# Order of gather, scatter, column copies and result scaling in the routed-expert loop of a hybrid encoder block

## The chip, the cores and the metric

One core of a Trainium2 chip runs the whole kernel. The metric is the device time in microseconds (us) of one execution: the median of three runs of the kernel before is 1347.29 us (1344.2 to 1349.36). One more execution was profiled; all rows below are of that one.

## The reference, cut to what matters

The block is one encoder layer on 512 tokens of width 1024 in float32: a token mixer (recurrent branch and differential attention) and then a mixture of experts (MoE). The change touches only the MoE. There each token is routed to 8 of 64 experts, and their weighted outputs are added up:

```python
    _, eidx = lax.top_k(sel, TOP_K)                      # 8 of 64 experts for each of 512 tokens
    w = jnp.take_along_axis(s, eidx, axis=-1)
    w = w / jnp.sum(w, axis=-1, keepdims=True) * ROUTED_SCALE
    gate = jnp.sum(jax.nn.one_hot(eidx, N_EXPERTS) * w[..., None], axis=1)
    ...
        hg = jnp.einsum('nd,edf->nef', tk, we_gate)      # 1024 -> 256
        hu = jnp.einsum('nd,edf->nef', tk, we_up)
        act = jax.nn.silu(hg) * hu * gk[..., None]
        return jnp.einsum('nef,efd->nd', act, we_down)   # 256 -> 1024
    ...
    ffn = routed + shared
    x = _layer_norm(ALPHA * x + g2[:, None, :] * ffn, ln2_g, ln2_b)
```

## The kernel before

The kernel computes only the (token, expert) pairs that were routed. They are packed into **units** of 128 rows (`Item` in the code): two halves of 64 rows, each half for one expert. Here there are 52 units, counted 0 to 51, and two units make a pair. Everything that has two buffers (`x_rows`, `y_item`, `row_index`, `y_index`, `places`, `columns`, `pick`) is used by even and odd units in turn.

What happens to unit i, engine by engine:

- GpSimd (POOL), `expert_columns` (L742, L743): copies the two experts' columns of the routing table (`places`, `columns`). The numbers of the experts come from the plan, read into registers by `Plan.move_on` (L420, L421) once for each pair.
- VectorE (DVE), `pick_tokens` (L2005): builds a 0/1 matrix that says which token sits in which row.
- TensorE (PE), `pick_slots` (L1118): multiplies it with the columns. This leaves in PSUM bank 7 the token number, the number of the result's row and the weight of each row.
- DVE, `token_index` (L2016): writes `row_index`. POOL, `gather` (L721): one indirect DMA brings the 128 token rows (4 KB each, 512 KB in all) from DRAM into `x_rows`.
- DVE, `token_weight` (L2026, L2027): copies the other numbers out of bank 7. Only then may PE run `pick_slots` of the next unit (semaphore `slots_read`), since it overwrites bank 7.
- PE, `transpose_rows` (L1127); ScalarE (ACT) takes the result out of PSUM; PE, `gate_up` (L1139); DVE, `activate` (L2048).
- DVE, `result_index` (L2054): writes `y_index`, the rows of DRAM that the results go to. As this buffer was last used by unit i-2, it waits until the scatter of unit i-2 has landed (semaphore `y_scattered`).
- PE, `project_down` (L1161); DVE, `result_out` (L2062): multiplies by g2 out of PSUM into `y_item`. POOL, `scatter` (L731): one indirect DMA writes the 128 result rows (512 KB) to DRAM.

The engines run these as a software pipeline. In step i (one turn of the loop) PE does, in this order: the transposes of the activations of unit i-1 (L1147), `pick_slots` of i+2, `transpose_rows` of i+1, `gate_up` of i, `project_down` of i-1. Each engine takes its instructions strictly in the order in which they are written, and waits where a semaphore isn't there yet. The orders around the change are written out by hand in the `step` functions of POOL (L763) and DVE (L2096); `over_items` (L457) calls them twice for each turn of a loop, an even unit and then an odd one. The loop's branch and `plan.move_on` stand ahead of the even unit.

The weights of the experts (3 MB each, 64 experts) come from DRAM through the queue of SyncE (SP), into a ring of four buffers. Gather and scatter both go through POOL's queue.

Of the kernel before, what the change touches and what calls it, by code (L numbers as in the profile page):

```python
# [119 lines left out]
def hybrid_block(nc, x, c, w_ada, b_ada, w_in, conv_w, conv_b, lru_w_a, lru_b_a, lru_w_i, lru_b_i, lru_lambda,  # L120
# [3 lines left out]
    with ctx:  # L124
# [255 lines left out]
        def bcast(row, at_axis, n):  # L380

            a = row.unsqueeze(at_axis)
            return a.broadcast_to([n if k == at_axis else d for k, d in enumerate(a.shape)])
# [57 lines left out]
        def wait(engine, semaphore, value):  # L441

            if not isinstance(value, int) or value > 0:
                engine.wait_ge(semaphore, value)

        def value_of(engine, value):

            return value if isinstance(value, int) else engine.snap(value)

        def count_of(engine, place, least, most):  # L450

            count, held = engine.alloc_register(f"count{place}"), engine.alloc_register(f"held{place}")
            engine.reg_load(held, items[0:1, place:place + 1])
            engine.reg_alu(count, held, least, ALU.max)
            return engine.snap(count, min_val=least, max_val=most)

        def over_items(engine, step, plan):  # L457


            pairs = count_of(engine, PAIRS, MIN_PAIRS, MAX_PAIRS)  # L460
            for par in range(2):
                step(Item(0, par, plan), par == 0, False, False)
            with engine.Fori(1, pairs - 1) as pair:
                if plan:
                    plan.move_on(pair)
                for par in range(2):
                    step(Item(pair, par, plan), False, False, False)
            if plan:
                plan.move_on(pairs - 1)
            for par in range(2):  # L470
                step(Item(pairs - 1, par, plan), False, par == 1, True)
            return Item(pairs - 1, 1, plan)
# [177 lines left out]
        def _(pool):  # L650
# [56 lines left out]
            def settle():  # L707

                pool.reg_alu(last_row, last_row, T - 1, ALU.min)
# [5 lines left out]
            def gather(item):  # L715
                indexed, transposed = value_of(pool, item.n + 1), value_of(pool, item.n - 1)
                pool.wait_ge(rows_stored, 16 * NT)
                wait(pool, index_ready, indexed)
                wait(pool, x_tr, transposed)
                settle()  # L720
                pool.indirect_dma_start(out=x_rows[item.par][:, :], out_offset=None, in_=u_rows,  # L721
                                        in_offset=bass.IndirectOffsetOnAxis(ap=row_index[item.par][:, 0:1], axis=0),
                                        bounds_check=last_row, oob_is_err=False).then_inc(rows_gathered[item.par], 16)

            def scatter(item):
                projected = value_of(pool, item.n + 1)
                pool.wait_ge(rows_stored, 16 * NT)
                wait(pool, yindex_ready, projected)
                wait(pool, y_out, projected)
                pool.reg_alu(last_result, last_result, T * TOPK - 1, ALU.min)  # L730
                pool.indirect_dma_start(out=y_rows, in_=y_item[item.par][:, :], in_offset=None,  # L731
                                        out_offset=bass.IndirectOffsetOnAxis(ap=y_index[item.par][:, 0:1], axis=0),
                                        bounds_check=last_result, oob_is_err=False
                                        ).then_inc(y_scattered[item.par], 16)

            def expert_columns(item):

                wait(pool, pick_done, item.n - 1)
                for h in range(2):
                    expert = item.expert(h)  # L740
                    settle()
                    nc.gpsimd.tensor_copy(places[item.par][:, :, h:h + 1], place[:, :, bass.ds(expert, 1)])  # L742
                    last = nc.gpsimd.tensor_copy(columns[item.par][:, :, h:h + 1, :], table[:, :, bass.ds(expert, 1), :])  # L743
                last.then_inc(columns_ready, 1)
# [9 lines left out]
            plan = Plan(pool, (ITEM_E,), 0, 4)  # L754
# [6 lines left out]
            expert_columns(Item(0, 2, plan))  # L761

            def step(item, first, last, end):  # L763
                if not end:

                    gather(item.ahead(2))
                    expert_columns(item.ahead(3))
                if not first and not (end and item.par):
                    scatter(item.ahead(-1))

            over_items(pool, step, plan)

            for t in range(NT - 1):
                last_rstd(2 * NT + t)
# [731 lines left out]
        def _(dve):  # L1506
# [493 lines left out]
            def pick_tokens(item):  # L2000

                wait(dve, columns_ready, item.n + 1)
                wait(dve, pick_done, item.n - 1)
                wait(dve, slot_step, item.n)
                V.tensor_tensor(pick[item.par][:, :, :].rearrange("p t (h s) -> p t h s", h=2),  # L2005
                                bcast(slot_id[:, :].rearrange("p (h s) -> p h s", h=2), 1, NT),
                                bcast(places[item.par][:, :, :], 3, HP), ALU.is_equal).then_inc(pick_ready, 1)
                wait(dve, pick_ready, item.n + 1)
                V.tensor_scalar(slot_id[:, :], slot_id[:, :], float(P), None, ALU.add).then_inc(slot_step, 1)

            def token_index(item):
                wait(dve, pick_done, item.n + 1)
                wait(dve, rows_gathered[item.par], item.pair * 16)
                for h in range(2):
                    rows = slice(h * HP, (h + 1) * HP)
                    last = V.tensor_scalar(row_index[item.par][rows, :], bank[7][rows, COLUMNS * h:COLUMNS * h + 1], float(SKIP),  # L2016
                                           None, ALU.add)
                last.then_inc(index_ready, 1)
# [14 lines left out]
            def take_gu(item):  # L2033
                wait(dve, gu_half, item.n * 2 - 1)
                for h in range(2):
                    load = item.load(h)
                    dve.wait_ge(gu_in[0], load * 32 + 32)
                    slot = slot_of(dve, slot_reg, load)
                    for b in range(2):
                        last = V.tensor_copy(gu_use[h][:, b, 0:KD // 2, :],  # L2040
                                             gu[:, bass.ds(slot, 1), b, 0:KD // 2, :].rearrange("p o k n -> p (o k) n"))
                    last.then_inc(gu_first, 1)

            def activate(item):

                wait(dve, silu_ready, item.n + 1)
                wait(dve, acted_tr, item.n)
                V.scalar_tensor_tensor(out=acted[:, :], in0=bank[item.par][:, DE:2 * DE],  # L2048
                                       scalar=picked[item.par][:, 1:2], in1=silu[:, :], op0=ALU.mult,
                                       op1=ALU.mult).then_inc(acted_ready, 1)  # L2050
# [6 lines left out]
            def result_out(item):  # L2057
                wait(dve, y_done, item.n + 1)
                wait(dve, y_scattered[item.par], item.pair * 16)
                for half in range(2):  # L2060
                    cols = slice(half * 512, (half + 1) * 512)
                    last = V.tensor_tensor(y_item[item.par][:, cols], bank[5 + half][:, :], g2_row[:, cols], ALU.mult)  # L2062
                last.then_inc(y_out, 1)
# [17 lines left out]
            plan = Plan(dve, (ITEM_L,), 0, 2)  # L2081
# [12 lines left out]
            shared_in_x1(1)  # L2094

            def step(item, first, last, end):  # L2096
                if not end:
                    token_index(item.ahead(2))
                    pick_tokens(item.ahead(3))
                if not last:  # L2100
                    take_gu(item.ahead(1))
                activate(item)
                result_index(item)
                if not end:
                    token_weight(item.ahead(2))
                if last:
                    scale_shared()
                if not first:
                    result_out(item.ahead(-1))

            last_item = over_items(dve, step, plan)
            wait(dve, y_done, last_item.n)
            load = last_item.load(1)
            dve.wait_ge(down_in, load * 16 + 16)
# [124 lines left out]
```

## Time and profile before

| | |
|---|---|
| median of three runs | 1347.29 us |
| the profiled execution | 1348.29 us |
| its span, first to last instruction | 1346.6 us |
| mean granted TensorE clock | 0.989 |
| units in the expert loop | 52 |
| PE busy in the span | 96% |
| DVE, ACT, POOL busy | 59%, 52%, 14% |

The loop over the experts fills the stretch from about 645 us to 1290 us. Times in the rows are microseconds from the start of the span; durations marked as a mean of one are nanoseconds. In a row of the timeline the bracket at the end tells how long the engine had been idle and who ended the wait. "issue" there is time of the engine's own sequencer: register work, reading the plan, a branch. PE's matrix products are pipelined and their ends are modelled, so that rows next to each other may overlap by some hundredths. For a DMA the landing is counted from the start of the instruction that issues it.

### The profile page before, as it was taken

The page shows a single profiled execution, that of the slowest core. Times are in us where ns is not written, and L with a number is a line of the kernel's source. Part 1 is how long each engine was busy: PE and PEld are TensorE (multiplying, and loading weights), DVE is VectorE, ACT ScalarE, POOL GpSimd, SP SyncE. Part 2 cuts the span into 40 slices and gives each one's busy share as a digit, 9 for nine tenths or more (in the row PEclk, how much of TensorE's full clock was granted, in tenths as well). Part 3 has the DMA queues.
Part 4 walks back from the last instruction along what each step waited for, and adds up shares of the span by engine and source line. Part 5 has one row for each costly group of instructions (what it writes and reads, how often), then busy time and mean ns, then how long its engine had stood idle before and what let it go on. Part 6 is the DMA issues. An engine that isn't in the chain of part 4 may idle for free.

```text
span 1346.6 us, 22140 instructions
## 1 busy us (share of the span) xinstructions
PE 1289.8 (96%) x6137; PEld 721.1 (54%) x6137; DVE 800.6 (59%) x1725; ACT 704.4 (52%) x938; POOL 188.0 (14%) x371
## 2 busy tenths in 40 slices
PE   2999999999999999999999999999999999999996
PEld 2778788877777778455343434333443343344332
DVE  6736777667888643587444545455455454454468
ACT  4346352334455322011577767777776777777711
POOL 1000000000111000121122122122221221222100
PEclk9899999999999999999999999999999999999998
DMA  8722446667531532534899999999999999998295
GB/s 325 227 75 97 142 152 227 204 227 252 188 126 32 187 140 74 185 137 163 282 310 353 346 387 403 354 384 395 384 332 385 364 398 389 363 399 334 99 385 235
DMA packets 131248, 351.53 MB, mean 261 GB/s; under 512 B 16222, under 2 KB 55255, under 8 KB 130178
## 3 DMA queue, kind: packets, MB, share of 16 engines
q1 hardware_dynamic: 112290, 300.93, 61.3%
q0 software_dynamic: 18912, 50.01, 10.0%
q8 instruction: 26, 0.43, 0.1%
q14 instruction: 20, 0.16, 0.0%
HBM read 323.97 MB, written 47.19 MB: 276 GB/s over the span
## 4 chain that ended last, share of the span: by engine, by line
PE 35%; DMA 10%; DVE 3%; issue 2%; POOLq 1%; DVEq 0%; POOL 0%; SPq 0%
PE bank L1139 20%; PE bank L1161 10%; DMA x_rows<-u_rows,row_index 7%; PE bank L1127 3%; DMA y_all<-y_rows 2%; DMA y_rows<-y_item,y_index 1%; DVE x L2146 1%; PE bank L1147 1%; POOLq L420 1%; PE bank L1118 1%; DVE y_item L2062 1%; DVEq L420 0%; DVE x L2200 0%; DVE x L2158 0%; DVE x L2181 0%
## 5 line engine op out<-in xcount | busy, mean ns | idle before, releaser
L1139 PE MATMUL bank<-gu_use,x_t 128*64 128x512 f32 x1664 | 369.7, 597 | 0.0
L1139 PEld LDWEIGHTS bank<-gu_use,x_t 128*64 128x64 f32 x1664 | 115.1, 137 | 217.5 <-issue 217.2
L1451 ACT ACTIVATE gu_use<-gu 128x1024 f32 x208 | 203.0, 1066 | 0.0
L1441 ACT ACTIVATE down_use<-down 128x2048 f32 x103 | 191.8, 1923 | 0.0
L829 PE MATMUL bank<-h_hi,w_lo 128*128 128x512 f32 x448 | 186.7, 417 | 1.8 <-DVE h_lo L1582 1.0
L1161 PE MATMUL bank<-down_use,act_t 128*64 128x512 f32 x832 | 187.4, 592 | 0.0
L830 PE MATMUL bank<-h_lo,w_hi 128*128 128x512 f32 x448 | 176.7, 394 | 0.0
L831 PE MATMUL bank<-h_hi,w_hi 128*128 128x512 f32 x448 | 176.6, 394 | 0.0
L2005 DVE TENSOR_TENSOR pick<-slot_id,places 128x512 fp32r<-128x512 f32 x53 | 36.7, 693 | 189.9 <-POOL columns L743 189.9
L1577 DVE TENSOR_TENSOR w_lo<-stream,w_hi 128x1024 fp32r<-128x1024 f32 x72 | 88.0, 1222 | 102.9 <-ACT w_hi L1250 102.8
L2040 DVE COPY gu_use<-gu 128x1024 f32 x208 | 130.0, 689 | 22.2 <-PE bank L1139 9.1
L1161 PEld LDWEIGHTS bank<-down_use,act_t 128*64 128x64 f32 x832 | 59.7, 137 | 119.0 <-issue 119.0
L731 POOL DMA_INDIRECT y_rows<-y_item,y_index x50 | 50.8, 1016 | 439.7 <-DVE y_item L2062 248.8
L1466 ACT ACTIVATE silu<-bank 128x256 f32<-128x256 f32 x52 | 20.0, 385 | 169.5 <-PE bank L1139 169.5
L2062 DVE TENSOR_TENSOR y_item<-bank,g_row 128x512 f32<-128x512 f32 x104 | 67.0, 686 | 62.4 <-PE bank L1161 62.4
L829 PEld LDWEIGHTS bank<-h_hi,w_lo 128*128 128x128 f32 x448 | 85.3, 190 | 27.3 <-issue 8.6
L831 PEld LDWEIGHTS bank<-h_hi,w_hi 128*128 128x128 f32 x448 | 85.2, 190 | 18.8
L830 PEld LDWEIGHTS bank<-h_lo,w_hi 128*128 128x128 f32 x448 | 85.4, 191 | 18.4 <-issue 2.6
L1250 ACT ACTIVATE w_hi<-stream 128x1024 fp32r<-128x1024 f32 x72 | 75.9, 1054 | 30.2 <-PE bank L831 25.6
L1127 PE MATMUL bank<-ident,x_rows 128*128 128x128 f32 x416 | 57.1, 281 | 7.0 <-DMA x_rows<-u_rows,row_index 6.8
L721 POOL DMA_INDIRECT x_rows<-u_rows,row_index x52 | 53.2, 1023 | 67.4 <-issue 52.3
L1459 ACT ACTIVATE x_t<-bank 128x512 f32<-128x512 f32 x104 | 56.2, 597 | 5.0 <-PE bank L1127 5.0
(312 smaller groups left out, 1599.3 us busy)
## 6 DMA issues: line engine op xcount, KB each, us to landing
gu<-in_we_gate SPq DMA_DIRECT2D x128, 512.0 KB, 6.4
gu<-in_we_up SPq DMA_DIRECT2D x128, 512.0 KB, 8.4
down<-in_we_down SPq DMA_DIRECT2D x64, 1024.0 KB, 8.6
stream<-in_w_in SPq DMA_DIRECT2D x28, 1024.0 KB, 5.7
ada_w<-in_w_ada POOLq DMA_DIRECT2D x8, 2048.0 KB, 9.6
y_rows<-zeros SPq DMA_DIRECT2D x8, 2048.0 KB, 11.6
y_all<-y_rows SPq DMA_DIRECT2D x8, 2048.0 KB, 17.1
ada_first<-in_w_ada SPq DMA_DIRECT2D x16, 512.0 KB, 10.5
```

The lines of the kernel that those rows point to most:

```text
L829: nc.tensor.matmul(o, w_lo[s][:, k, :], hi[:, k, :], start=(k == 0), stop=False)
L830: nc.tensor.matmul(o, w_hi[s][:, k, :], lo[:, k, :], start=False, stop=False)
L831: last = nc.tensor.matmul(o, w_hi[s][:, k, :], hi[:, k, :], start=False, stop=(k == KD - 1))
L1127: last = nc.tensor.transpose(bank[2 + k // 4][:, k % 4 * P:(k % 4 + 1) * P], x_rows[item.par][:, k * P:(k + 1) * P], ident[:, :])
L1139: last = nc.tensor.matmul(bank[item.par][rows, :], x_t[:, k, rows], gu_use[h][:, :, k, :], start=(k == 0), stop=(k == KD - 1))
L1161: last = nc.tensor.matmul(bank[5 + half][rows, :], act_t[:, f, rows], down_use[h][:, f, cols], start=(f == 0), stop=(f == FE - 1))
L1250: nc.scalar.activation(w_hi[n % 2][:, :, :], stream_of(group), ACT.Copy).then_inc(whi_ready, 1)
L1441: nc.scalar.activation(down_use[h][:, :, :], down[:, bass.ds(slot, 1), :, :].rearrange("p o k n -> p (o k) n"), ACT.Copy).then_inc(down_ta ...
L1451: last = nc.scalar.activation(gu_use[h][:, b, KD // 2:KD, :], gu[:, bass.ds(slot, 1), b, KD // 2:KD, :] .rearrange("p o k n -> p (o k) n") ...
L1577: V.tensor_tensor(w_lo[n % 2][:, :, :], stream_of(group), w_hi[n % 2][:, :, :].bitcast(F32), ALU.subtract).then_inc(wlo_ready, 1)
L2040: last = V.tensor_copy(gu_use[h][:, b, 0:KD // 2, :], gu[:, bass.ds(slot, 1), b, 0:KD // 2, :].rearrange("p o k n -> p (o k) n"))
L2062: last = V.tensor_tensor(y_item[item.par][:, cols], bank[5 + half][:, :], g2_row[:, cols], ALU.mult)
```

## The change

On POOL, step i did gather of i+2, column copies for i+3, scatter of i-1. Now it does gather of i+2, scatter of i-2, then (for even units) the plan reads, then the column copies for i+3. On DVE, the multiplication by g2 of the unit before stood last in the step; now it stands behind `token_index` in the next step. No instruction of the loop is added or dropped.

```diff
@@ gpsimd
             def step(item, first, last, end):
+                early = isinstance(item.n, int) and item.n < 2
                 if not end:
-
                     gather(item.ahead(2))
-                    expert_columns(item.ahead(3))
-                if not first and not (end and item.par):
-                    scatter(item.ahead(-1))
-
-            over_items(pool, step, plan)
+                if not early:
+                    scatter(item.ahead(-2))
+                if not end:
+                    if item.par == 0 and not first:
+                        plan.move_on(item.base)
+                    expert_columns(Item(item.base, item.offset + 3, plan))
+
+            over_items(pool, step, None)
@@ vector
             def step(item, first, last, end):
+                early = isinstance(item.n, int) and item.n < 2
                 if not end:
                     token_index(item.ahead(2))
+                if not early:
+                    result_out(item.ahead(-2))
+                if not end:
                     pick_tokens(item.ahead(3))
                 if not last:
                     take_gu(item.ahead(1))
...
                 if last:
                     scale_shared()
-                if not first:
-                    result_out(item.ahead(-1))
 
             last_item = over_items(dve, step, plan)
+            result_out(last_item.ahead(-1))
```

POOL inside the loop, from the scatter that stands at the end of the even step into the odd step, before. The last number of a name is its buffer (`x_rows_186`, `y_item_183` belong to odd units).

```order
L730 REGISTER_ALU [waits y_out,yindex_ready,rows_stored]
L731 DMA y_rows<-y_item_183,y_index_198 4096x1024
L444 REGISTER_ALU [waits rows_stored]
L709 REGISTER_ALU [waits x_tr,index_ready]
L721 DMA x_rows_186<-u_rows,row_index_196 128x1024
L439 ISA [waits pick_done]
L742 COPY places_199<-place 128x4
```

The same place on POOL, now:

```order
L444 REGISTER_ALU [waits rows_stored]
L709 REGISTER_ALU [waits x_tr,index_ready]
L721 DMA x_rows_186<-u_rows,row_index_196 128x1024
L730 REGISTER_ALU [waits y_out,yindex_ready,rows_stored]
L731 DMA y_rows<-y_item_183,y_index_198 4096x1024
L439 ISA [waits pick_done]
L742 COPY places_199<-place 128x4
```

Gather and scatter have changed places; they are issued one right behind the other in both.

POOL at the head of the loop (the even step), now; before, the plan reads (L420, L421) stood between the scatter at the end of the turn and this gather.

```order
L444 ISA [waits rows_stored]
L444 REGISTER_ALU [waits index_ready]
L709 REGISTER_ALU [waits x_tr]
L721 DMA x_rows_185<-u_rows,row_index_195 128x1024
L444 REGISTER_ALU [waits rows_stored]
L730 REGISTER_ALU [waits y_out,yindex_ready]
L731 DMA y_rows<-y_item_182,y_index_197 4096x1024
L435 ISA
L420 TENSOR_LOAD items
```

The plan reads now stand behind both DMAs, ahead of the column copies alone.

DVE at the seam of the even and the odd step, before:

```order
L2054 TENSOR_SCALAR y_index_197<-picked_193 128x1 [waits y_scattered0]
L2026 COPY picked_193<-bank 64x1 [waits pick_done,yindex_ready]
L2027 TENSOR_SCALAR picked_193<-bank 64x1
L2026 COPY picked_193<-bank 64x1
L2027 TENSOR_SCALAR picked_193<-bank 64x1
L444 ISA [waits y_done]
L2062 TENSOR_TENSOR y_item_183<-bank,g_row 128x512 [waits y_scattered1]
L2062 TENSOR_TENSOR y_item_183<-bank,g_row 128x512
L2016 TENSOR_SCALAR row_index_196<-bank 64x1 [waits rows_gathered1,pick_done]
L2016 TENSOR_SCALAR row_index_196<-bank 64x1
```

The same place on DVE, now (the lines are three further down in the file):

```order
L2057 TENSOR_SCALAR y_index_197<-picked_193 128x1 [waits y_scattered0]
L2029 COPY picked_193<-bank 64x1 [waits pick_done,yindex_ready]
L2030 TENSOR_SCALAR picked_193<-bank 64x1
L2029 COPY picked_193<-bank 64x1
L2030 TENSOR_SCALAR picked_193<-bank 64x1
L2019 TENSOR_SCALAR row_index_196<-bank 64x1 [waits rows_gathered1,pick_done]
L2019 TENSOR_SCALAR row_index_196<-bank 64x1
L2065 TENSOR_TENSOR y_item_183<-bank,g_row 128x512 [waits y_scattered1,y_done]
L2065 TENSOR_TENSOR y_item_183<-bank,g_row 128x512
```

The two writes of the row index have moved ahead of the two multiplications.

## Rows read from the trace of the kernel before

**Rows 1.** Page, part 1: busy time, share of the span, instructions.

```profile
PE 1289.8 (96%) x6137; PEld 721.1 (54%) x6137; DVE 800.6 (59%) x1725; ACT 704.4 (52%) x938; POOL 188.0 (14%) x371
```

**Rows 2.** Stretch of the loop: us; busy of PE, PEld, DVE, ACT, POOL; clock; DMA share; GB/s.

```profile
940.00:1000.00 60.00, 59.53 (x306) 23.95 (x304) 28.09 (x76) 45.05 (x50) 13.14 (x30) 1.00 0.98 364
```

**Rows 3.** Timeline of PE, two steps (28, 29): start us, us, what.

```profile
993.46 0.59 PE L1118 MATMUL bank<-columns,pick 128*128 128x8 f32 x4
...
994.92 7.09 PE L1139 MATMUL bank<-gu_use,x_t 128*64 128x512 f32 x32
...
1005.57 0.59 PE L1118 MATMUL bank<-columns,pick 128*128 128x8 f32 x4
```

**Rows 4.** Chain of waits that ended last: start us, us, what.

```profile
674.84 7.02 PE bank L1139 x32
...
973.77 7.97 DMA x_rows<-u_rows,row_index
...
1167.85 9.75 DMA y_rows<-y_item,y_index
1178.56 0.58 PE bank L1118 x4
...
1252.77 7.02 PE bank L1139 x32
```

**Rows 5.** Waits, 640 to 1290 us: total us, times, longest us.

```profile
PE bank L1127 <- DMA x_rows<-u_rows,row_index: 6.8, 9, 1.2
...
DVE y_index L2054 <- DMA y_rows<-y_item,y_index: 4.9, 8, 1.1
...
PE bank L1118 <- DVE picked L2027: 0.8, 2, 0.5
```

**Rows 6.** Timeline of DVE, the same steps.

```profile
993.38 1.29 DVE L2062 TENSOR_TENSOR y_item<-bank,g_row 128x512 f32<-128x512 f32 x2 [1.83 <-PE bank L1161]
995.86 0.33 DVE L2016 TENSOR_SCALAR row_index<-bank 64x1 int32<-64x1 f32 x2 [1.19 <-issue]
...
1004.16 0.14 DVE L2054 TENSOR_SCALAR y_index<-picked 128x1 int32<-128x1 f32 x1
...
1004.72 0.23 DVE L2027 TENSOR_SCALAR picked<-bank 64x1 f32<-64x1 f32 x1
```

**Rows 7.** Timeline of POOL, the same steps.

```profile
995.57 1.02 POOL L731 DMA_INDIRECT y_rows<-y_item,y_index  x1 [9.36 <-DVE y_item L2062]
998.25 1.02 POOL L721 DMA_INDIRECT x_rows<-u_rows,row_index  x1 [1.66 <-issue]
999.28 0.19 POOL L742 COPY places<-place 128x4 f32 x1
...
1007.79 1.01 POOL L731 DMA_INDIRECT y_rows<-y_item,y_index  x1 [7.92 <-DVE row_index L2016]
1009.11 1.02 POOL L721 DMA_INDIRECT x_rows<-u_rows,row_index  x1 [0.31 <-issue]
```

**Rows 8.** Timeline, the last prologue step: an index that waits for PE, a gather for it.

```profile
658.53 0.58 PE L1118 MATMUL bank<-columns,pick 128*128 128x8 f32 x4 [0.35 <-DVE picked L2027]
659.15 0.32 DVE L2016 TENSOR_SCALAR row_index<-bank 64x1 int32<-64x1 f32 x2 [0.76 <-PE bank L1118]
660.29 1.01 POOL L721 DMA_INDIRECT x_rows<-u_rows,row_index  x1 [7.37 <-DVE row_index L2016]
```

**Rows 9.** Line L731, all scatters.

```profile
L731 POOL DMA_INDIRECT y_rows<-y_item,y_index x50: 988/1016/1034, 675.4 to 1277.2; - x50
...
DMA to landing us min/median/max: 3.0/7.2/9.8
```

**Rows 10.** Line L731, the one scatter at 1007.79.

```profile
DMA to landing us min/median/max: 7.2/7.2/7.2
```

**Rows 11.** Line L721, the one gather at 1009.11.

```profile
DMA to landing us min/median/max: 8.6/8.6/8.6
```

**Rows 12.** Line L721, all gathers, 640 to 1290 us.

```profile
DMA to landing us min/median/max: 5.3/7.8/9.5
```

**Rows 13.** Waits of SP's queue, 640 to 1290 us: total us, times, longest.

```profile
SPq L444 <- DMA gu<-in_we_up: 69.4, 39, 4.5
SPq L590 <- ACT down_use L1441: 59.5, 15, 10.3
```

## The prediction

> **What bounds the kernel now.** I read the shares of busy time first: PE is busy for 96% of the span, no other engine over 59% [rows 1]. So only what makes PE wait in the expert loop, or lets it wait less, counts. The stretch in the middle of the loop says two things: PE is busy for 59.5 of 60 us, and the DMA engines are at 0.98 of their time, 364 GB/s [rows 2]. What is issued as a DMA therefore lands slowly, and its landing will vary.
>
> The timeline of PE gives the length of a step: from one L1118 to the next 1005.57 - 993.46 = 12.11 us, in a step in which PE waited for nothing [rows 3]. The chain of waits shows where steps are longer. The L1139 groups of unit 2 and unit 49 start at 674.84 and 1252.77 [rows 4]: 577.9 us for 47 steps, and 47 x 12.11 = 569.2, so 8.7 us were lost in waits. The chain names two kinds. One is a gather that lands late (as the 7.97 us at 973.77). The other is a scatter that lands late: issued at 1167.85, it takes 9.75 us, and PE's L1118 starts behind it at 1178.56 [rows 4]. The list of waits has the first as 6.8 us of PE in 9 waits, one of them in the prologue, and the second as 0.8 us in 2 [rows 5]. Step by step, from the starts of L1139, I count 12 late gathers for 8.0 us and one late scatter for 0.7 us. Ten of the 12 are gathers of even units.
>
> Why a late scatter reaches PE: `result_index` waits for the scatter of two units ago, `token_weight` stands behind it on DVE, and PE's next L1118 waits for `token_weight`. DVE needs from y_index at 1004.16 to the end of L2027 at 1004.95 [rows 6]; in the chain L1118 starts 0.96 us after the scatter's landing at 1177.60 [rows 4]. So a scatter has to land 0.95 us before the next L1118.
>
> **The change part by part.** I count from P, the start of L1118 in a step (993.46 even, 1005.57 odd) [rows 3].
>
> *Row index first, gather first.* Before, the even gather goes at 998.25, P + 4.8, the odd one at 1009.11, P + 3.5 [rows 7]. In between lie the two multiplications (1.29 us), 1.19 us of plan reading on DVE [rows 6], the scatter (1.02 us) and 1.66 us of sequencer time on POOL, 1.35 us more than the 0.31 us of the odd step [rows 7]. Now DVE waits for L1118 alone: the prologue shows that case, index at L1118 + 0.62 (658.53 to 659.15), 0.32 us long, gather 0.82 us after its end [rows 8]. So both gathers go at about P + 1.8, 3.0 us and 1.7 us earlier. DVE's plan reads in the even step now run while it would wait for PE anyway (1.83 us idle before y_item [rows 6]). All 12 waits for a gather are under 1.4 us, and the gather has no scatter in front of it any more: they all go, -8.0 us.
>
> *Scatter second.* Before, it goes at P + 2.1 (even) and P + 2.2 (odd) [rows 3, 7]. Now y_item starts behind the index, at P + 0.95, ends at P + 2.24, and with the 0.90 us that POOL took before (994.67 to 995.57 [rows 6, 7]) the scatter could go at P + 3.14. The gather ends at P + 2.8, and 0.31 us later is P + 3.1: the same. So every scatter is issued 1.0 us later. It must land by P + 12.11 - 0.95, so it had about 9.0 us for landing and has 8.0 us now. The wait that this makes stands at the head of PE's step: transposes, gate_up and project_down are all behind it, so it is paid in full, in every step in which it comes.
>
> *How long the scatter takes to land now* is what the trace before doesn't show. All scatters: median 7.2 us, most 9.8 [rows 9]; of 50, seven took 8.0 us or more when read one at a time. But these had POOL's queue to themselves; now each stands 1.3 us behind a gather of 512 KB. The nearest rows are the odd gathers before, each 1.3 us behind a scatter in the same queue: scatter at 1007.79 landed after 7.2 us, gather at 1009.11 after 8.6 us [rows 10, 11]. I read the 24 such pairs of the loop one at a time: the gathers' landings have a median of 8.05 us and a mean of 7.9, and in 11 of the 24 pairs the second DMA lands 2.4 to 2.7 us after the first, though issued only 1.3 us later. So the second of a close pair does wait for the first. Bounds for the cost in the 48 steps:
> - lower: the scatter lands as now, whatever is ahead of it. The excess over 8.0 us, summed over the scatters of before, is 4 us.
> - middle: it lands as the odd gathers did. 12 of 24 are over 8.0 us, 8.4 us together, so 16.8 us for 48 steps.
> - upper: the gather, which alone takes 7.7 us (the median of the even ones; 7.8 over all [rows 12]), lands first and the scatter 2.5 us behind it: 7.7 + 2.5 - 1.3 = 8.9 us. The excess over 8.0 us is then 0.9 us a step and a little more for the spread, 44 us.
>
> I take the middle, for it is the pair in the same queue at the same distance, with only the order turned.
>
> The Trainium skill bears on this, "DMA: Bandwidth & Descriptors", section "Queues, rings and completion order": on one DMA engine the descriptors of one ring are taken in ring order, and the semaphore's increment lands only after every earlier write of that engine. By that the scatter's landing can't come before the gather's, which agrees with the 24 pairs and speaks for the middle or the upper bound. Its section "SWDGE vs HWDGE vs iDMA" says that within a queue descriptors only start in order and that reading and writing are separate sides; by that the scatter would lose little behind a gather, and the sum would be the lower bound. Which holds for this order no row here shows.
>
> *Plan reads.* On POOL they now stand between scatter and column copies: scatter ends at P + 4.1, + 1.35 us gives copies at P + 5.5; before it was 999.28, P + 5.8 [rows 7]. Nothing, and there is room: DVE's pick matrix feeds a product a whole step later. On DVE they hurt only when the odd step is late: then 1.19 us [rows 6] follow `token_weight` where otherwise 0.15 + 0.62 us pass, so the next scatter is 0.4 us later. In half of 24 steps, half of it felt: 2.5 us.
>
> *Ends of the loop.* The last two steps issue no gather, and the last scatter still goes when y_item of unit 49 is done; the tail is as before: nothing.
>
> Sum against the profiled execution: 1348.3 - 8.0 - 0.7 (the old scatter wait is counted anew) + 16.8 + 2.5 = 1358.9 us. That execution is 1.0 us above the median of the runs, so 1358 us.
>
> **Rivals.**
> 1. *The scatter doesn't feel the gather (not slower).* Landing as before: -8.7 + 4 + 0.5 (fewer late odd steps) = -4.2, 1343 us. For it: a gather reads DRAM and a scatter writes it, and a slower PE loads the DMA less. Against: the 2.5 us spacing of the pairs. It decides from a landing of 8.0 us: only if the median scatter falls to under about 7.3 us is the kernel not slower.
> 2. *The scatter queues behind the whole gather.* Upper bound: 1347.3 - 8.7 + 44 + 2.5 = 1385 us. For it: gathers alone take 7.7 us, scatters 7.2. Against: odd gathers behind a scatter should then have shown 8.4 us and showed 8.05; and a loop that is 3% longer eases the DMA.
> 3. *The gathers' time is hidden anyway.* With DMA at 0.98 the weights would come late instead, and the 8 us would be given back; with the scatter as in rival 1 that is about 1347 + 4 = 1351 us, no change. Against: SP's queue waited 59.5 us for ACT to free a buffer [rows 13], so the weights run ahead; for it the 69.4 us in which it waited for earlier loads [rows 13].
> 4. *The waits of the gathers stay*, because the index comes no sooner: then 1347.3 + 18 = 1365 us; the prologue speaks against it [rows 8].
>
> **How the numbers follow.** Of a measurement of this kernel only more than 0.5% (6.7 us, under 1340.6 or over 1354.0) can be told from no change. My forecast, with landings of 7.8 to 8.4 us, has 0.38 and a range of its own of 1350 to 1369. Rival 1 has 0.29, rival 2 0.18, rival 3 0.10, rival 4 0.05. Faster is the part of rival 1 where landings get shorter even than now, 0.12. No change is the rest of it, 0.17, most of rival 3, 0.08, and the low end of the forecast, 0.06: 0.31. Slower: 0.57. For 8 in 10 the range goes from 1340 to 1380: about 0.11 lies below, and the upper half of rival 2, 0.09, above.
>
> **What will show it.** In the profile after: PE's waits for `x_rows` are gone from the loop, and the chain no longer has them; gathers go about 1.8 us after L1118; scatters go 3.1 us after it, 1.3 us behind the gather; their landing has a median near 8 us; DVE's y_index waits for `y_rows` in about half of the steps, and L1118 waits for `picked`. Steps without such a wait still take 12.11 us. I am wrong if the scatters' median is still near 7.2 us, or if scatters go less than 2.5 us after L1118: then most of the 8 us is kept.

## The result, and the profile after

| | median us | runs | ratio to before, 95% interval |
|---|---|---|---|
| before | 1346.66 | 1344.2 to 1349.36 (4) | 1 |
| changed | 1382.60 | 1378.08 to 1388.73 (4) | 1.0269 (1.0225 to 1.0314) |

The change makes the kernel 2.7% slower, by 36 us. I had forecast slower, at 1358 us, with a range from 1340 to 1380: the side was right, the size was not. The profiled execution took 1388.73 us, its span is 1387.0 us, so it is 6 us above the median of its own runs; against the span before it is 40.4 us longer.

The list of waits of the changed kernel, 640 to 1330 us (total us, times, longest us). Lines of PE and DVE are three higher than before (L1121 is the slot product, L1130 the transposes of `x_rows`, L1142 gate_up); those of POOL are the same.

```profile
POOL x_rows L721 <- PE bank L1130: 318.7, 34, 11.6
...
DVE y_index L2057 <- DMA y_rows<-y_item,y_index: 74.9, 36, 4.7
...
PE bank L1121 <- DVE picked L2030: 30.5, 23, 2.9
...
DVE row_index L2019 <- issue: 18.7, 10, 1.9
```

PE's wait for `x_rows`, 6.8 us before [rows 5], has no row any more: the gathers are early. DVE's wait for the scatter went from 4.9 to 74.9 us and PE's wait for `picked` from 0.8 to 30.5 us [rows 5]. The chain of waits of the changed kernel (part 4 of its page) says the same; before, the gather had 7% of the span in it and the scatter 1%:

```profile
DMA y_rows<-y_item,y_index 18%; PE bank L1142 13%; PE bank L832 9%; PE bank L834 9%; PE bank L833 9%; PE bank L1164 6%; PE bank L1000 4%; PE bank L1130 3%; PE bank L1031 2%; PE bank L898 2%; PE bank L1215 1%; PE bank L1121 1%; DVE acc_first L1563 1%; PE bank L922 1%; POOL x_rows L721 1%
```

All scatters of the changed kernel, against [rows 9]:

```profile
L731 POOL DMA_INDIRECT y_rows<-y_item,y_index x50: 983/1006/1033, 674.8 to 1315.2; - x50
...
DMA to landing us min/median/max: 2.1/8.2/11.0
```

One bad step shows the whole mechanism. First DVE (start us, us, what, idle before):

```profile
798.34 0.15 DVE L2057 TENSOR_SCALAR y_index<-picked 128x1 int32<-128x1 f32 x1 [2.24 <-DMA y_rows<-y_item,y_index]
...
798.91 0.23 DVE L2030 TENSOR_SCALAR picked<-bank 64x1 f32<-64x1 f32 x1
801.00 0.32 DVE L2019 TENSOR_SCALAR row_index<-bank 64x1 int32<-64x1 f32 x2 [1.87 <-issue]
801.36 1.29 DVE L2065 TENSOR_TENSOR y_item<-bank,g_row 128x512 f32<-128x512 f32 x2
...
813.30 0.15 DVE L2057 TENSOR_SCALAR y_index<-picked 128x1 int32<-128x1 f32 x1 [3.25 <-DMA y_rows<-y_item,y_index]
```

Then POOL in the same step:

```profile
802.18 1.03 POOL L721 DMA_INDIRECT x_rows<-u_rows,row_index  x1 [10.84 <-DVE row_index L2019]
803.52 1.01 POOL L731 DMA_INDIRECT y_rows<-y_item,y_index  x1 [0.30 <-issue]
```

And PE:

```profile
799.19 0.61 PE L1121 MATMUL bank<-columns,pick 128*128 128x8 f32 x4 [0.24 <-DVE picked L2030]
...
811.13 0.44 PE L1150 MATMUL bank<-ident,acted 128*128 128x128 f32 x2
814.24 0.58 PE L1121 MATMUL bank<-columns,pick 128*128 128x8 f32 x4 [2.67 <-DVE picked L2030]
...
815.70 8.78 PE L1142 MATMUL bank<-gu_use,x_t 128*64 128x512 f32 x32
```

The step before ended late: a scatter held y_index until 798.34. So DVE came to its plan reads (1.87 us "issue") only at 799.14, when the slot product had nearly started; the row index is written at 801.00, 1.81 us after L1121 instead of 0.7. The reads themselves are no slower than before. Line L420 on DVE's sequencer, in the step of [rows 6] in the kernel before and in this step (durations in ns: shortest, median, longest; first and last start):

```profile
L420 DVEq TENSOR_LOAD <-items x4: 302/306/309, 994.0 to 995.3; - x4
```

```profile
L420 DVEq TENSOR_LOAD <-items x4: 302/304/308, 799.1 to 800.5; - x4
```

Before, they began while the multiplications (993.38 to 994.67) still ran, and only their last 1.19 us showed as idle time. Here nothing runs beside them, and all of the 1.87 us shows. Gather and scatter go 1.1 us later for it, the scatter 1.34 us behind the gather. It lands after 9.8 us, DVE waits 3.25 us, PE 2.67 us, and the step takes 814.24 - 799.19 = 15.05 us instead of 12.11. A third thing follows: the next gate_up takes 8.78 us where it took 7.09 [rows 3]. The stretches of that step, of the next, and of a part of the next, same columns as [rows 2]:

```profile
799.00:814.20 15.20, 12.38 (x62) 4.88 (x62) 6.29 (x17) 11.59 (x14) 2.63 (x6) 1.00 1.01 364
814.24:828.00 13.76, 13.76 (x61) 5.19 (x62) 6.16 (x16) 6.05 (x8) 2.62 (x6) 0.88 0.99 366
...
815.86:819.27 3.41, 3.41 (x10) 0.96 (x10) 0.89 (x3) 0.96 (x1) 2.62 (x6) 0.50 1.00 335
```

The granted clock of PE was 1.00 in the step with the wait. In the step behind it, which had no wait and took 1.65 us more, it was 0.88 in the mean: 0.50 (1.2 GHz) for 3.4 us, 1.6 us after the wait had ended, and 1.00 (2.4 GHz) for the rest.

From unit 2 to unit 49 the loop took 617.8 us, of which 47 x 12.11 are 569.2: 48.6 us lost, against 8.7 before. Read step by step, as what each step takes beyond 12.11 us, 36.0 us are waits at L1121 (the 30.5 us of the list are PE's idle time alone), and 12.6 us are seven steps in which PE ran slower, each behind a wait of 1.6 to 3.2 us. At the longest of these the clock fell 1.1 us before the wait ended (at 1051.38, L1121 starts at 1052.43). Not every such wait did it: one of 2.62 us had none behind it. 48.6 - 8.7 = 39.9 us is nearly all of the 40.4 us between the spans.

### The profile page after: what moved, and what is told of

Its sections match the earlier page's. It is cut to its first block, busy times and chain, and to the rows that moved or that the text cites. A ratio compares the mean times of both kernels' runs of the same rounds, so it can differ in the third digit from the quotient of the medians.

```text
span 1387.0 us, 22158 instructions
## 1 busy us (share of the span) xinstructions
PE 1307.4 (94%) x6137; PEld 726.4 (52%) x6137; DVE 803.6 (58%) x1725; ACT 704.1 (51%) x938; POOL 187.9 (14%) x371
## 4 chain that ended last, share of the span: by engine, by line
PE 66%; DMA 20%; DVE 6%; issue 4%; DVEq 1%; POOL 1%; ACT 1%; POOLq 0%; SPq 0%; ACTq 0%
DMA y_rows<-y_item,y_index 18%; PE bank L1142 13%; PE bank L832 9%; PE bank L834 9%; PE bank L833 9%; PE bank L1164 6%; PE bank L1000 4%; PE bank L1130 3%; PE bank L1031 2%; PE bank L898 2%; PE bank L1215 1%; PE bank L1121 1%; DVE acc_first L1563 1%; PE bank L922 1%; POOL x_rows L721 1%
## 5 line engine op out<-in xcount | busy, mean ns | idle before, releaser
L1142 PE MATMUL bank<-gu_use,x_t 128*64 128x512 f32 x1664 | 378.2, 608 | 0.0
L1142 PEld LDWEIGHTS bank<-gu_use,x_t 128*64 128x64 f32 x1664 | 116.9, 140 | 224.6 <-issue 224.3
L721 POOL DMA_INDIRECT x_rows<-u_rows,row_index x52 | 53.6, 1031 | 491.3 <-PE bank L1130 318.7
L2019 DVE TENSOR_SCALAR row_index<-bank 64x1 int32<-64x1 f32 x104 | 16.2, 156 | 78.9 <-PE bank L1121 59.5
L1121 PE MATMUL bank<-columns,pick 128*128 128x8 f32 x208 | 31.5, 257 | 30.5 <-DVE picked L2030 30.5
L1130 PE MATMUL bank<-ident,x_rows 128*128 128x128 f32 x416 | 59.2, 288 | 0.0
## 6 DMA issues: line engine op xcount, KB each, us to landing
y_rows<-zeros SPq DMA_DIRECT2D x8, 2048.0 KB, 12.6
```

The lines of the kernel that those rows point to most:

```text
L1130: last = nc.tensor.transpose(bank[2 + k // 4][:, k % 4 * P:(k % 4 + 1) * P], x_rows[item.par][:, k * P:(k + 1) * P], ident[:, :])
L1142: last = nc.tensor.matmul(bank[item.par][rows, :], x_t[:, k, rows], gu_use[h][:, :, k, :], start=(k == 0), stop=(k == KD - 1))
```

## The experiments

Theory A was the forecast's mechanism: a step costs what the scatter's issue after the slot product, its landing and 0.95 us of DVE come to beyond 12.11 us, and the landing is later because the gather stands ahead in the same queue. Each row of results is a median with the ratio to the kernel before, run on the same chip (its medians there: 1346.02 us for e1 to e4, 1346.72 us for e5 to e7).

### e1: the scatter ahead of the gather again

```diff
@@ gpsimd, step
-                if not end:
-                    gather(item.ahead(2))
                 if not early:
                     scatter(item.ahead(-2))
                 if not end:
+                    gather(item.ahead(2))
```

> The changed kernel with GpSimd's scatter put ahead of the gather again; DVE's order stays as changed, so the scatter is still issued about 3.1 us after TensorE's slot product. Theory A (most of the loss is that the scatter stands behind the gather in GpSimd's queue and lands later, which DVE's result index and through it TensorE wait for): the scatter's median landing falls from 8.1 to 8.6 us to about 7.2 us, TensorE's waits at the slot product fall from about 36 us to some 5 us, the gathers now go at about 4.5 us and some land late as before the change (8 to 16 us), in all 1350 to 1362 us. Theory B (the later issue of the scatter by 1 us is enough, the order in the queue does nothing): the waits at the slot product stay at 30 us or more, landings stay over 8 us, and with the late gathers it is 1385 to 1395 us.

1357.27 us, 1.0084 (1.0051 to 1.0116). All scatters, and the waits:

```profile
DMA to landing us min/median/max: 2.2/7.1/8.5
```

```profile
PE bank L1129 <- DMA x_rows<-u_rows,row_index: 10.7, 16, 1.2
DVE y_index L2056 <- DMA y_rows<-y_item,y_index: 9.9, 17, 1.2
...
PE bank L1120 <- DVE picked L2029: 1.0, 3, 0.4
```

And two steps of POOL (L1120 of PE starts at 984.82 and 996.71 here):

```profile
987.76 1.01 POOL L731 DMA_INDIRECT y_rows<-y_item,y_index  x1 [9.42 <-DVE y_item L2064]
989.08 1.02 POOL L721 DMA_INDIRECT x_rows<-u_rows,row_index  x1 [0.31 <-issue]
...
999.97 1.02 POOL L731 DMA_INDIRECT y_rows<-y_item,y_index  x1 [9.26 <-DVE y_item L2064]
1001.30 1.02 POOL L721 DMA_INDIRECT x_rows<-u_rows,row_index  x1 [0.31 <-issue]
```

The scatter still goes about 3.2 us after the slot product, 1.0 us later than before the change, but it lands after a median of 7.1 us again, none over 8.5 (the profile has the landings of 25 of the 50 scatters, those of even units), and DVE waits for no scatter, even or odd, longer than 1.2 us. PE's wait at the slot product is 1.0 us instead of 30.5. So theory B, that the later issue is enough, falls. The queue's order is the cause of the late landing. What e1 still loses is mostly the other DMA: every gather now goes at 4.5 us or later, behind the scatter, and PE waits for 16 of them. Behind one such wait, of 1.23 us, the clock fell to 0.50 here too, and that step took 1.7 us more.

### e2: DVE's plan reads moved into idle time

```diff
@@ vector, step
+                item = Item(item.base, item.offset, plan)
...
                 if not early:
                     result_out(item.ahead(-2))
+                if item.par == 0 and not first:
+                    plan.move_on(item.base)
                 if not end:
                     pick_tokens(item.ahead(3))
...
-            last_item = over_items(dve, step, plan)
+            last_item = over_items(dve, step, None)
+            last_item = Item(last_item.base, last_item.offset, plan)
```

> The changed kernel with DVE's plan reads put behind the multiplications by g2 in the even step, where DVE waits for the column copies anyway. Theory A (a late odd step exposes 1.9 us of DVE's plan reads and delays the next even gather and scatter; this was 12 us of the loss by the rows): the even row index always starts about 0.7 us after the slot product, even scatters go at 3.2 us instead of a median of 3.9, and the time falls by 12 to 18 us to 1365 to 1371 us. Theory C (that delay only shifts a wait that the landing makes anyway): 1378 to 1384 us.

1363.93 us, 1.0139 (1.0109 to 1.0169): 19 us less than the changed kernel (18 if each is taken against its own runs of the kernel before), 1 us below the expected 1365 to 1371. The waits, and all scatters:

```profile
DVE y_index L2057 <- DMA y_rows<-y_item,y_index: 78.6, 41, 3.9
PE bank L1121 <- DVE picked L2030: 16.0, 22, 1.9
```

```profile
DMA to landing us min/median/max: 2.1/8.2/10.2
```

The scatters have the same median landing as in the changed kernel (8.2 us), but none is issued late any more: read one at a time, the even ones go at 3.25 us with no exception over 3.5. Theory C falls. With each scatter's own issue time, issue + landing + 0.95 - 12.11, where positive, adds up to 23.8 us over the 47 steps, and the steps lost 22.0 us in waits: the sum over a step holds. The loop lost 25.5 us here, 23 less than in the changed kernel. Of the 23, 9 are the clock: only two steps behind a wait ran slower (3 us), against seven. Another 5 are landings that happened to be less late (21.7 us beyond 8.0 us, against 26.4), and 9 are left for the delay by the plan reads. That the shorter waits are why the clock fell less often is likely, not shown: the two waits behind which it fell here were of 1.6 and 1.7 us, and one of 2.1 us had no fall behind it.

### e5: GpSimd's part alone

The `step` of POOL is that of the changed kernel, everything on DVE that of before.

> Only GpSimd's part of the change (gather, scatter of two units behind, plan reads, column copies); DVE's order is that of before, so the multiplications by g2 and, in the even step, the plan reads stand ahead of the row index. Theory A (the time is the scatter's issue after the slot product, plus its landing behind the gather, plus 0.95 us, over 12.11 us): the gather goes at about 2.4 us (odd) and 3.6 us (even), the scatter at 3.7 and 4.9 us, later than in the changed kernel, with landings of 8 us or more; so it is slower than the changed kernel, 1395 to 1420 us. Rival (the two parts of the change add up: e1 showed 11 us for DVE's part, which leaves 25 us for GpSimd's): 1367 to 1375 us.

1414.39 us, 1.0508 (1.0470 to 1.0545). The additive rival (1367 to 1375) falls. The sum over one step, with each scatter's own issue and landing, gives 63.6 us of waits, where the steps that ran at full clock lost 54.0; the rest of what the loop lost, some 20 us, is slower clock, for which theory A has no term. Its waits:

```profile
DVE y_index L2057 <- DMA y_rows<-y_item,y_index: 94.9, 41, 4.2
PE bank L1121 <- DVE picked L2030: 48.3, 30, 3.3
```

The two parts do not add up, for DVE's part made GpSimd's less bad: it brings the row index, and so both DMAs, forward. With DVE's old order the scatter goes at a median of 3.5 (odd) and 4.75 us (even), the landing has the same median of 8.2 us as in the changed kernel, and the loop lost 77.3 us, some 20 of them by a slower clock in ten steps.

### e6: a gather of a quarter of the rows

```diff
-            pool.reg_mov(last_row, T - 1)
+            pool.reg_mov(last_row, T // 4 - 1)
```

> The changed kernel in which the gather brings only rows of the first 128 tokens (the other rows, three quarters on the average, are left out, so that x_rows is mostly old data); issue times and all instructions stay. Theory A (the scatter lands late because 512 KB of the gather are ahead of it in the same queue): the scatter's median landing falls from 8.1 to 8.6 us to 7.2 us or less though it is issued at the same place, and the time falls to 1345 to 1355 us. Rival (the scatter is slow at this moment of the step whatever stands ahead of it): landings stay at 8 us and the time at 1375 us or more. Leaving out 20 MB of reads also unloads the DMA engines by some 8%, which helps both a little.

1353.50 us, 1.0053 (1.0032 to 1.0074). All scatters:

```profile
DMA to landing us min/median/max: 2.1/7.2/9.4
```

```profile
DVE y_index L2057 <- DMA y_rows<-y_item,y_index: 46.9, 34, 3.0
PE bank L1121 <- DVE picked L2030: 10.2, 10, 2.4
```

Same instructions, the same issue times after a step in time, fewer bytes ahead of the scatter: the landing goes from 8.2 back to 7.2 us and 29 of the 36 us are gone. What e1 did by the order this does by the size. That the gather's bytes are also missing from the load of the DMA engines isn't separated here; e1, with all bytes there, is free of that.

### e3, e4, e7: nothing waits for the scatter

The wait exists only because `y_index` has two buffers and is written early. In e3 the row number is kept in a column of its own for each unit, and `y_index` is written just ahead of the multiplications, one step later:

```diff
+        y_num = at("y_num", 2.25, [P, 2 * MAX_PAIRS + 4])
@@ token_weight
-                wait(dve, yindex_ready, item.n - 1)
+                wait(dve, acted_ready, item.n - 1)
...
-                    V.tensor_copy(picked[item.par][rows, 0:1], bank[7][rows, col + 1:col + 2])
+                    V.tensor_copy(y_num[rows, bass.ds(item.n, 1)], bank[7][rows, col + 1:col + 2])
@@ result_index
-                V.tensor_scalar(y_index[item.par][:, :], picked[item.par][:, 0:1], float(SKIP), None, ALU.add
+                wait(dve, slots_read, item.n + 1)
+                V.tensor_scalar(y_index[item.par][:, :], y_num[:, bass.ds(item.n, 1)], float(SKIP), None, ALU.add
@@ result_out
+                result_index(item)
                 wait(dve, y_done, item.n + 1)
@@ step
                 activate(item)
-                result_index(item)
```

> The changed kernel, but the number of the result's row is kept in a column of its own for each unit, and y_index is written just ahead of the multiplications by g2, so that nothing in the step waits for the scatter of two units ago. Theory A: DVE's wait for y_rows and TensorE's wait at the slot product vanish though the scatters land as late as in the changed kernel, the gathers stay early, the granted clock stays at 1.00, steps are 12.11 us, and it is 1334 to 1340 us, faster than both kernels. Theory D (the DMA engines are full, and a loop without waits would wait for the weights instead): waits of DVE for the weights grow to 8 us or more and it is 1345 us or above.

1342.55 us, 0.9971 (0.9952 to 0.9989), ten runs from 1335.88 to 1344.05. The scatters of e3:

```profile
DMA to landing us min/median/max: 2.1/8.5/10.7
```

They land later than in any other kernel here and cost nothing: in the profiled execution (1336.37 us) all 47 steps took 12.11 us, at a granted clock of 1.00. The median of its runs is above the 1334 to 1340 us that theory A gave, below the 1345 us of theory D, and 6 us above that execution, so other executions have lost something in a place that I haven't seen. The mean granted clock doesn't explain it (0.993 in a run of 1343.92 us, 0.990 in the one of 1336.37); that stays open.

e4 is the same edit on the kernel before.

> The kernel before with the same edit as e3 (number of the result's row kept for each unit, y_index written ahead of the multiplications by g2). Theory A: in the old order this wait cost only 0.7 us, and the 8 us of late gathers stay: 1344 to 1348 us. Rival: the wait costs the old order more than the rows show; then 1338 to 1341 us.

1346.10 us, 1.0002 (0.9985 to 1.0019). In the old order the wait for the scatter cost nothing that can be measured, as its 0.7 us in the rows said; the rival falls. In its profiled execution (1343.11 us) the loop still lost 5.1 us, and PE still waited for gathers.

e7 is e3 with the edit of e2.

> The changed kernel with both edits: the number of the result's row kept for each unit (as in e3), and DVE's plan reads behind the multiplications (as in e2). Theory A: with no late step there is nothing for the plan reads to delay, so it is the same as e3, 1338 to 1344 us, with no wait for gathers or scatters in the loop. If some executions of e3 do have late steps (its runs spread from 1336 to 1344 us), this edit would take them away, and the median would be 1336 to 1338 us.

1338.86 us, 0.9953 (0.9934 to 0.9971), twelve runs: faster than both kernels, by 7.9 us or 0.5% against before, and 3.7 us under e3, which ran on another chip. Their intervals against before overlap, so that e7 is faster than e3 is likely but not shown. The chain of waits of e7 at unit 2 and unit 49 (start us, us, what):

```profile
672.20 7.02 PE bank L1143 x32
...
1241.52 7.02 PE bank L1143 x32
```

569.3 us for 47 steps, against 577.9 before [rows 4]: the loop loses 0.1 us. The waits of e7 hold no `x_rows` on PE and no `y_rows` on DVE. What is left of PE's wait at the slot product is one wait, in the prologue, and the weights hardly come late (L1122 is the slot product here, L2044 DVE's copy of the weights):

```profile
DVE gu_use L2044 <- DMA gu<-in_we_up: 6.1, 16, 2.7
...
PE bank L1122 <- DVE picked L2031: 0.3, 1, 0.3
```

So the 8.7 us that the change was able to win are there to be had, once the wait for the scatter is out of the way, and theory D (full DMA engines would turn them into waits for the weights) falls.

## Why the prediction was wrong in size

What held, point by point:

- *Gathers early.* Forecast at 1.8 us after the slot product; they go at 1.7 (odd) and, where the step before was in time, 1.9 us (even); in 13 of the 24 even steps it wasn't, and they go at up to 3.0 us. All waits for `x_rows` went, -8.0 us as forecast.
- *Scatters 1.0 us later, with 8.0 us left.* Forecast 3.1 us; measured 3.15 (odd) and 3.25 us (even in time). The 0.95 us from landing to slot product held (813.32 to 814.24).
- *The wait for the scatter is paid in full by PE.* Held: 22.0 us of PE's waits for a sum of 23.8 us in e2.
- *Which bound for the landing.* The middle case, the landing of the odd gathers, was nearly right as a mean: 8.0 us over 47 scatters against 7.9 assumed. Rival 1 fell by e1 and e6. Rival 2 gave the time, 1385 us, but by luck. Its picture was right, for in all 48 pairs the scatter landed behind its gather. Its size was not: 8.9 us in the median and 44 us in all, against 8.5 us (over the 47 scatters of the loop; 8.2 over all 50) and 26.4 us. What it had too much there stood in for the two terms below that it had too small or not at all. Its 7.7 us for a gather alone came from even gathers, and these went 2.7 us behind a scatter that had not landed yet; ahead of the scatter the gathers took 7.2 us in the mean. Rival 4 fell with the waits for `x_rows`, and rival 3 with e7.

The steps that failed are three terms of the sum:

| term | forecast us | measured us, by the steps of the profiled execution |
|---|---|---|
| old losses gone (gathers, one scatter) | -8.7 | -8.7 |
| landing beyond 8.0 us | +16.8 | +26.4 |
| plan reads of DVE behind a late odd step | +2.5 | about +10 |
| slower clock behind a wait | none | +12.6 |
| sum | +10.6 | +40 |

The other three executions took 1378.1 to 1383.1 us, 6 to 11 us less than this one; how their losses divide was not profiled.

- *Landing beyond 8.0 us.* The 26.4 us are the sum over 47 scatters of 3.13 + landing + 0.95 - 12.11, where positive. With nearly the same mean the spread was wider: 27 of 47 took 8.0 us or more, up to 11.0, where the 24 gathers had ended at 9.5. What counts is the mean of the excess, and near the bound that grows with the spread.
- *Plan reads.* I took the 1.19 us of idle time in [rows 6] for the length of the reads. It was only what stuck out behind the multiplications; the reads take 1.87 us, and behind a late odd step all of it shows. I had the next scatter 0.4 us later for it, in half of 24 steps, and half of that felt. It went up to 1.1 us later, in 13 even steps, and it doesn't stop at one step: the later scatter is the next late one. Waits at L1121 are 36.0 us in all, so 9.6 us are left to this. That is a remainder; e2, which removes the delay, leaves 9 us to it by the same account, and is 19 us faster with what it saves in landings and clock.
- *The clock.* I had none of it. In the rows before, no wait in the loop was over 1.4 us, and one gate_up in the prologue was slow; I did not ask what a wait of 3 us would do. Seven waits of 1.6 to 3.2 us cost 12.6 us beyond themselves, by stretches of 3.4 to 6.8 us at 1.2 GHz. In the loops of e3 and e7, without such waits, the granted clock stayed at 1.00.

One cause lies under the second and the third: I priced each step on its own, with the delays independent. In a loop where the lateness of one step makes the next one later, the steps that are over the bound pay several times. It does not lie under the first: in e2, where no step delays the next issue, the landings beyond 8.0 us still come to 21.7 us against the 16.8 forecast, and why their spread was wider than that of the odd gathers is open. e5 was forecast after this was seen, and its 1414 us lie within 1395 to 1420; but theory A's sum there has no term for the clock, and the 20 us that the clock took lie within the width of that range.

On the rule named in the prediction: the scatter behind a gather of 512 KB landed after a median of 8.2 us, against 7.1 us ahead of it (e1) and 7.2 behind a quarter of it (e6). In all 48 pairs of the changed kernel it landed after the gather, by a median of 2.2 (odd) and 2.35 us (even), though issued 1.3 to 1.4 us after it. This agrees with the Trainium skill, "DMA: Bandwidth & Descriptors", section "Queues, rings and completion order": on one DMA engine a ring's descriptors are taken in ring order, and the semaphore's increment lands only after every earlier write of that engine. The page says this of the queues of SP and ACT; gather and scatter here go through GpSimd's. That reading and writing are separate sides, as its section "SWDGE vs HWDGE vs iDMA" says, did not keep the scatter from being delayed.

## What to carry to other kernels

When two DMAs share a queue, don't ask only which one is waited for today: write down for each how long it has from issue to the point where its landing stops an engine, and put first the one with less room. Better still, look at what makes a landing count at all. Here it was a two-buffer index tile written earlier than needed, and moving that write took away the price of putting the scatter second. The order still counted: with the same edit the old order stayed at 1346 us (e4), for it still issues its even gathers 4.7 us or more after the slot product.

A landing whose median lies at its bound costs more than its mean says: add the spread, the work that was hidden only because everything was in time, and what TensorE can lose in clock behind a wait.

## What the runs showed of the hardware that I had not expected

- A wait of PE of 1.6 to 3.2 us can cost as much again: the granted clock fell to 0.50 (1.2 GHz) for 3.4 us, and the following step took 13.76 us with no wait in it, instead of 12.11. It happened behind seven waits in the changed kernel, two in e2, two in e6, ten in e5, and in e1 behind one of 1.2 us. It did not happen behind others of up to 2.6 us in the changed kernel and 2.8 us in e5, so the length of the wait alone doesn't decide it.
- Removing three quarters of a gather that nobody waited for was worth 29 us (e6), most of it, by e1, because something else stood behind it in its queue.
- Four small register reads of the plan, 0.30 us each, take 1.9 us of DVE's sequencer with their moves and clamps. They run while an instruction before them still works: before, 0.7 us of them lay beside the multiplications and 1.2 us showed as idle [rows 6]. Nothing in the busy shares shows them.
